# A recurrence's triangular inverse: levels one to four in 32x32 blocks, the last level as one corner block

## What is computed

```python
def wkv7_scan(r, decay, k, v, a_vec, b_vec):
    # S_t = S_{t-1} diag(w_t) + (S_{t-1} a_t) b_t^T + v_t k_t^T ;  y_t = S_t r_t
    def step(S, inp):
        r_t, w_t, k_t, v_t, a_t, b_t = inp
        sa = jnp.einsum('bhvk,bhk->bhv', S, a_t)
        S = S * w_t[:, :, None, :] + sa[..., :, None] * b_t[..., None, :] + v_t[..., :, None] * k_t[..., None, :]
        y = jnp.einsum('bhvk,bhk->bhv', S, r_t)
        return S, y
```

## Time and profile before

| | |
|---|---|
| median of 3 runs | 3347.98 us (3345.4 to 3358.46) |
| profiled execution, span from first to last instruction | 3342.9 us |
| the recurrence within it | 1762 to 2157 us |
| busy over the span: PE, DVE, ACT, POOL | 3046.9, 2026.2, 1103.6, 88.7 us |
| matmul records | 19562 |

### The profile page before, as it was taken

The page is one execution under the profiler, slowest core; times in us unless marked ns, Lnnn a source line. Parts: engine busy times, 40 slices in busy tenths (PEclk is TensorE's granted clock), DMA queues, the critical chain, the costliest instruction groups (busy, mean ns, idle before and its releaser), DMA issues.

```text
span 3342.9 us, 45792 instructions
## 1 busy us (share of the span) xinstructions
PE 3046.9 (91%) x19562; PEld 2487.4 (74%) x19565; DVE 2026.2 (61%) x3130; ACT 1103.6 (33%) x1684; POOL 88.7 (3%) x100
## 2 busy tenths in 40 slices
PE   6998899998998898995989888889999999889999
PEld 5876787786766787883767778768888777678887
DVE  5856795876577794876426777655353354554353
ACT  2334331223255431222324333342122444442121
POOL 0000000000000000000001121100000001000000
PEclk8998999998998999997999887889999999999999
DMA  8761453534621444541220000213332221023222
GB/s 238 170 182 35 166 195 133 189 129 148 204 75 45 170 158 143 178 153 51 84 46 10 12 7 12 70 62 101 101 95 94 77 88 51 7 76 101 95 94 88
DMA packets 236399, 345.55 MB, mean 103 GB/s; under 512 B 19604, under 2 KB 121948, under 8 KB 236196
## 3 DMA queue, kind: packets, MB, share of 16 engines
q1 hardware_dynamic: 217780, 327.27, 30.5%
q10 hardware_dynamic: 18416, 15.36, 1.7%
HBM read 340.45 MB, written 2.15 MB: 102 GB/s over the span
## 4 chain that ended last, share of the span: by engine, by line
PE 70%; DVE 18%; ACT 5%; DMA 5%; issue 1%; SPq 0%; DVEq 0%; ACTq 0%
PE bank L141 68%; DVE w_tiles L150 3%; DVE w_low L150 3%; DVE ada_acc L162 2%; PE bank L144 2%; ACT w_high L147 1%; DMA weight_ring<-in_f_w_down 1%; DMA first_ada<-in_w_ada 1%; ACT stage L147 1%; DVE x_natural L150 1%; DVE u_low L150 1%; DMA weight_ring<-in_d_w_in 1%; DMA weight_ring<-in_f_w_up 1%; DVE x_natural L162 1%; DVE stage L150 1%
## 5 line engine op out<-in xcount | busy, mean ns | idle before, releaser
L150 DVE TENSOR_TENSOR w_low<-weight_ring,w_high 128x2048 fp32r<-128x2048 f32 (+2 forms) x212 | 463.9, 2188 | 605.4 <-ACT w_high L147 605.4
L147 ACT ACTIVATE w_high<-weight_ring 128x2048 fp32r<-128x2048 f32 (+2 forms) x212 | 388.2, 1831 | 768.7 <-DMA weight_ring<-in_mlp_down 171.6
L141 PE MATMUL bank<-u_high,w_high 128*128 128x512 f32 x1472 | 582.9, 396 | 16.0 <-DVE u_low L150 5.9
L141 PE MATMUL bank<-u_high,w_low 128*128 128x512 f32 x1472 | 575.5, 391 | 0.0
L141 PE MATMUL bank<-u_low,w_high 128*128 128x512 f32 x1472 | 575.4, 391 | 0.0
L141 PE MATMUL bank<-w_high,u_high 128*128 128x512 f32 x896 | 354.0, 395 | 11.6 <-DVE u_low L150 6.7
L141 PE MATMUL bank<-w_low,u_high 128*128 128x512 f32 x896 | 350.4, 391 | 0.0
L141 PE MATMUL bank<-w_high,u_low 128*128 128x512 f32 x896 | 350.3, 391 | 0.0
L141 PEld LDWEIGHTS bank<-u_high,w_high 128*128 128x128 f32 x1472 | 278.0, 189 | 87.3 <-DVE u_low L150 19.1
L141 PEld LDWEIGHTS bank<-u_high,w_low 128*128 128x128 f32 x1472 | 277.7, 189 | 59.0
L141 PEld LDWEIGHTS bank<-u_low,w_high 128*128 128x128 f32 x1472 | 278.2, 189 | 55.8
(11 more groups left out here) (387 smaller groups left out, 4326.7 us busy)
## 6 DMA issues: line engine op xcount, KB each, us to landing
ada_ring<-in_mod_w SPq DMA_DIRECT2D x48, 1024.0 KB, 7.5
weight_ring<-in_f_w_up SPq DMA_DIRECT2D x44, 1024.0 KB, 5.1
ada_ring<-in_w_ada SPq DMA_DIRECT2D x40, 1024.0 KB, 7.3
weight_ring<-in_mlp_up SPq DMA_DIRECT2D x32, 1024.0 KB, 5.4
weight_ring<-in_mlp_down SPq DMA_DIRECT2D x32, 1024.0 KB, 5.0
weight_ring<-in_f_w_down SPq DMA_DIRECT2D x24, 768.0 KB, 4.7
weight_ring<-in_m_w_in SPq DMA_DIRECT2D x16, 1024.0 KB, 9.7
weight_ring<-in_d_w_in SPq DMA_DIRECT2D x12, 1024.0 KB, 5.3
```

The lines of the kernel that those rows point to most:

```text
L141: return self.e.matmul(out, l, r, start=start, stop=stop, skip_group_check=True)
L147: return self.e.activation(out, in_, f, **kw) if self.live else QUIET
L150: return self.e.tensor_tensor(out, a, b, op) if self.live else QUIET
```

## The change

Two facts of block matrices are used. The blocks of levels 0 to 4 never cross a border of 32 positions, so up to level 4 N, W and T hold nothing outside the diagonal 32x32 blocks. And level 5 joins two finished 32x32 blocks of a chunk by a single block, the upper right corner, which is all that is not zero in it.

After the change T, W, X, Bl and the masks are 32 columns wide instead of 64 (SB = 32), one 32x32 block in each strip of 32 partitions. A new tile `near` holds the diagonal blocks of N; DVE gathers it from G1 in two operations (the second half's columns times a column mask, then the first half's added). Levels 0 to 4 use `near`. A product of a level is sixteen matmuls of 32x32x32, `strips`, each on a diagonal strip of the array; the transposition t0 likewise. At level 5, PE multiplies the corner of G1 by T, from the lower strip of a chunk to the upper (`edges`, eight matmuls), and then X by W back. POOL places the 32x32 blocks of W into a tile `full` of 64 columns with zeros beside them, and DVE adds the corner to it. `w gh` reads `full`. POOL makes one mask fewer for each head and this placing instead. The number of steps in every generator, and so the order of the lists, stays as it was. `wkv_constants` has 708 columns instead of 834.

```diff
+SB = 32
+W_CONST = 3 * P + 8 * SB + HD + 4
...
+    strip = row // SB * SB + np.arange(SB)[None, :]
     up = []
-    for lv in range(6):
+    for lv in range(5):
         b = 1 << lv
         pair = (row // (2 * b) == col // (2 * b))
-        up.append(pair & (col % (2 * b) >= b) & (row % (2 * b) < b))
+        up.append(np.take_along_axis(pair & (col % (2 * b) >= b) & (row % (2 * b) < b), strip, axis=1))
     fold = lambda x: np.where(row[:, :] < CH, x[:, 0:CH], x[:, CH:P])
     stack = (row % HD == np.arange(HD)[None, :])
+    first, second = row % CH < SB, row % CH >= SB
+    halves = [np.repeat(first, SB, axis=1), np.repeat(second, SB, axis=1), first, second]
+    eye = (row % SB == np.arange(SB)[None, :])
     chunk = (row // CH == np.arange(2)[None, :])
-    wkv = [upto, same] + [fold(x) for x in [before, upto] + up] + [stack, chunk]
+    wkv = [upto, same] + [fold(x) for x in [before, upto]] + up + halves[0:2] + [eye, stack, chunk] + halves[2:4]
...
-        halves = lambda tile: (tile[:, 0:TT * CH], tile[:, TT * CH:])
+        parts = lambda tile: [chunks(tile[:, j * TT * SB:(j + 1) * TT * SB]) for j in range(4)]
         w.heads = []
         for h in range(2):
-            (T, W), Bl = halves(next(take)), halves(next(take))
-            w.heads.append(dict(G1=self.w_g[:, h, 0], G2=self.w_g[:, h, 1], T=chunks(T), W=chunks(W), Bl=[chunks(x) for x in Bl],
-                                X=next(take), R2=next(take)))
+            first, second = next(take), next(take)
+            T, W = parts(first)[0:2]
+            Bl, near = parts(second)[0:2], parts(second)[2]
+            w.heads.append(dict(G1=self.w_g[:, h, 0], G2=self.w_g[:, h, 1], T=T, W=W, Bl=Bl, near=near,
+                                full=chunks(first[:, TT * CH:]), X=next(take), R2=next(take)))
...
+        at = 3 * P
+        w.up = [cst[:, at + l * SB:at + (l + 1) * SB] for l in range(5)]
+        w.place, w.eye = cst[:, at + 5 * SB:at + 7 * SB], cst[:, at + 7 * SB:at + 8 * SB]
+        at += 8 * SB
+        w.stack, w.chunk = cst[:, at:at + HD], cst[:, at + HD:at + HD + 2]
+        w.first, w.second = cst[:, at + HD + 2:at + HD + 3], cst[:, at + HD + 3:at + HD + 4]
...
+        strips = [(t, slice(q, q + SB), slice(t * SB, t * SB + SB)) for t in range(TT) for q in range(0, P, SB)]
+        edges = [(t, slice(q, q + SB), slice(q + SB, q + 2 * SB), slice(t * SB, t * SB + SB)) for t in range(TT) for q in (0, CH)]
         for h, hd in enumerate(w.heads):
             pe.wait_ge(self.V, "w w", p, h, 0)
             if h in self.free:
                 pe.wait_ge(*self.free[h])
-            for t, c, at in blocks:
-                m = pe.matmul(self.bank[h][c, at], hd["W"][c, t, :], self.ident[c, c], True, True)
+            for t, r, at in strips:
+                m = pe.matmul(self.bank[h][r, at], hd["W"][r, t, :], self.ident[r, r], True, True)
             m.then_inc(*self.T.up("w t0", p, h))
             self.free[h] = (self.A, "w t0", p, h)
             yield
...
                     pe.wait_ge(self.V, "w t", p, h, l - 1)
-                pe.wait_ge(self.G, "w bl", p, h, l)
                 pe.wait_ge(*self.free[6 + h])
-                for t, c, at in blocks:
-                    m = pe.matmul(self.bank[6 + h][c, at], hd["Bl"][l % 2][c, t, :], hd["T"][c, t, :], True, True)
+                if l < 5:
+                    pe.wait_ge(self.G, "w bl", p, h, l)
+                    for t, r, at in strips:
+                        m = pe.matmul(self.bank[6 + h][r, at], hd["Bl"][l % 2][r, t, :], hd["T"][r, t, :], True, True)
+                else:
+                    pe.wait_ge(self.V, "w w", p, h, 4)
+                    for t, lo, hi, at in edges:
+                        m = pe.matmul(self.bank[6 + h][hi, at], hd["G1"][lo, t, 0, SB:CH], hd["T"][lo, t, :], True, True)
                 m.then_inc(*self.T.up("w x", p, h, l))
                 self.free[6 + h] = (self.A, "w x", p, h, l)
                 yield
             for h, hd in enumerate(w.heads):
-                X = chunks(hd["X"][:, 0:TT * CH])
+                X = chunks(hd["X"][:, 0:TT * SB])
                 pe.wait_ge(self.A, "w x", p, h, l)
                 pe.wait_ge(self.V, "w w", p, h, l - 1)
                 if l < 5:
                     pe.wait_ge(*self.free[h])
-                    for t, c, at in blocks:
-                        m = pe.matmul(self.bank[h][c, at], hd["W"][c, t, :], X[c, t, :], True, True)
+                    for t, r, at in strips:
+                        m = pe.matmul(self.bank[h][r, at], hd["W"][r, t, :], X[r, t, :], True, True)
                     m.then_inc(*self.T.up("w tx", p, h, l))
                     self.free[h] = (self.V, "w t", p, h, l)
-                for t, c, at in blocks:
-                    m = pe.matmul(self.bank[6 + h][c, at], X[c, t, :], hd["W"][c, t, :], True, True)
+                    for t, r, at in strips:
+                        m = pe.matmul(self.bank[6 + h][r, at], X[r, t, :], hd["W"][r, t, :], True, True)
+                else:
+                    for t, lo, hi, at in edges:
+                        m = pe.matmul(self.bank[6 + h][lo, at], X[hi, t, :], hd["W"][hi, t, :], True, True)
                 m.then_inc(*self.T.up("w wx", p, h, l))
                 self.free[6 + h] = (self.V, "w w", p, h, l)
...
-                m = pe.matmul(self.bank[h][c, ts(t)], hd["W"][c, t, :], hd["R2"][c, ts(t)], True, True)
+                m = pe.matmul(self.bank[h][c, ts(t)], hd["full"][c, t, :], hd["R2"][c, ts(t)], True, True)
...
-            a.activation(hd["T"], chunks(self.bank[h][:, 0:TT * CH]), ACT.Copy).then_inc(*self.A.up("w t0", p, h))
...
-                a.activation(hd["X"][:, 0:TT * CH], self.bank[6 + h][:, 0:TT * CH], ACT.Copy).then_inc(*self.A.up("w x", p, h, l))
...
-            v.tensor_tensor(hd["W"], hd["G1"][:, :, 0, :], spread(w.up[0]), ALU.mult).then_inc(*self.V.up())
+            v.tensor_scalar(hd["near"], hd["G1"][:, :, 0, SB:CH], w.second, None, ALU.mult).then_inc(*self.V.up())
             v.wait_ge(self.V)
-            v.tensor_tensor(hd["W"], hd["W"], spread(w.stack), ALU.add).then_inc(*self.V.up("w w", p, h, 0))
+            v.scalar_tensor_tensor(hd["near"], hd["G1"][:, :, 0, 0:SB], w.first, hd["near"], ALU.mult, ALU.add).then_inc(
+                *self.V.up("w near", p, h))
+            v.wait_ge(self.V)
+            if p:
+                v.wait_ge(self.G, "w full", p - 1, h)
+            v.tensor_tensor(hd["W"], hd["near"], spread(w.up[0]), ALU.mult).then_inc(*self.V.up())
+            v.wait_ge(self.V)
+            v.tensor_tensor(hd["W"], hd["W"], spread(w.eye), ALU.add).then_inc(*self.V.up("w w", p, h, 0))
             yield
...
-                    v.tensor_tensor(hd["T"], hd["T"], chunks(self.bank[h][:, 0:TT * CH]), ALU.add).then_inc(*self.V.up("w t", p, h, l))
+                    v.tensor_tensor(hd["T"], hd["T"], chunks(self.bank[h][:, 0:TT * SB]), ALU.add).then_inc(*self.V.up("w t", p, h, l))
                 v.wait_ge(self.T, "w wx", p, h, l)
                 v.wait_ge(self.V)
-                v.tensor_tensor(hd["W"], hd["W"], chunks(self.bank[6 + h][:, 0:TT * CH]), ALU.add).then_inc(*self.V.up("w w", p, h, l))
+                step = chunks(self.bank[6 + h][:, 0:TT * SB])
+                if l < 5:
+                    v.tensor_tensor(hd["W"], hd["W"], step, ALU.add).then_inc(*self.V.up("w w", p, h, l))
+                else:
+                    v.wait_ge(self.G, "w full", p, h)
+                    corner = hd["full"][:, :, SB:CH]
+                    v.scalar_tensor_tensor(corner, step, w.first, corner, ALU.mult, ALU.add).then_inc(*self.V.up("w w", p, h, l))
...
         for h, hd in enumerate(w.heads):
-            g.wait_ge(self.V, "w w", p, h, 0)
-            g.tensor_tensor(hd["Bl"][1], hd["G1"][:, :, 0, :], spread(w.up[1]), ALU.mult).then_inc(*self.G.up("w bl", p, h, 1))
+            g.wait_ge(self.V, "w near", p, h)
+            g.tensor_tensor(hd["Bl"][1], hd["near"], spread(w.up[1]), ALU.mult).then_inc(*self.G.up("w bl", p, h, 1))
             yield
         for l in range(1, 6):
             for h, hd in enumerate(w.heads):
-                if l < 5:
+                if l < 4:
                     if l > 1:
                         g.wait_ge(self.T, "w x", p, h, l - 1)
-                    elif p:
+                    g.tensor_tensor(hd["Bl"][(l + 1) % 2], hd["near"], spread(w.up[l + 1]), ALU.mult).then_inc(
+                        *self.G.up("w bl", p, h, l + 1))
+                elif l == 5:
+                    if p:
                         g.wait_ge(self.T, "w gh", p - 1, h)
-                    g.tensor_tensor(hd["Bl"][(l + 1) % 2], hd["G1"][:, :, 0, :], spread(w.up[l + 1]), ALU.mult).then_inc(
-                        *self.G.up("w bl", p, h, l + 1))
+                    g.wait_ge(self.V, "w w", p, h, 4)
+                    g.tensor_tensor(hd["full"].rearrange("p t (b s) -> p t b s", b=2),
+                                    hd["W"].unsqueeze(2).to_broadcast([P, TT, 2, SB]),
```

(14 more changed lines are left out.)

## The result

The changed kernel takes 3376.03 us (median of 4, 3374.53 to 3381.69) against 3346.69 for the kernel before (4 runs): ratio 1.0092, 95% interval 1.0075 to 1.0108. It is slower by 0.9%, where 0.9% faster was forecast, and lies above the forecast's range.

The account below looks back on a forecast made before the run. PE and DVE alternate: PE bounds levels 1 and 4 at 1.2 GHz, DVE most of the rest. Terms summed to 3.7 us a pair, 30 us for eight, giving 3318 us (chance 0.62); own range 3302 to 3337, overall 3302 to 3350.

Parts of the forecast that it names:

- Unit prices: PE in the recurrence: a burst of 32x32x32 products takes 0.27 us at 2.4 GHz, 0.45 at 1.2 GHz.
- rival (c): PE's bursts: matmuls start no faster than 29 ns apart, however small; a pair 3.8 us slower, 3378 us; chance 0.07.
- A change of shape: PE between state products and inverse: 0.1 us each, 14 added a pair, 5 on the path, 0.5 us.
- DVE's additions and its masking: DVE in a middle pair: 128x128 additions at 286 ns; masking, four operations of 128x128 for two of 128x256, loses 0.75 us.
- rival (d): DVE: 128x128 costs nearly what 128x256 does; 1.3 us gained a pair, 3338 us; chance 0.22 together with rival (a).
- columns halve: PE's bursts: halved columns, twice as many products side by side and doubled number give half the time if nothing else limits.
- Instructions: PE in the recurrence: 6656 more instructions; 7 us if issue waits grew with them, taken as 0, 7 kept for upper end.
- Rival (b): Score products and pair's end: clock stays low, 13 us more a pair, in half of the pairs; 3370 us; chance 0.09.
- Level 1: Level 1 of a middle pair, at 1.2 GHz: sums start 2.0 us earlier, 1.2 us of it kept as gain.
- rival (a): Each pair: one more 3.4 us stretch at 1.2 GHz; 1.5 us gain stays, 3336 us; chance 0.22 together with rival (d).
- The sum: Recurrence: terms of a middle pair add to 3.7 us gained, eight pairs 30 us, 3318 us of time.

Follow-up runs that it names:

- The split: Kernel before, each 64x64x64 product of t0 and levels 1 to 4 split into two of 64x32x64: 3369.36 us, 1.0065; with idle products, 3338.37 us, 0.9992.
- the fillers: Idle bf16 128x128x512 products where PE waits in the recurrence: added to the changed kernel 3373.45 us, 1.0085; to the kernel before 3311.19 us, 0.9903.
- its pair: Kernel before, inverse products in one pass of upper halves, with idle products: 3321.33 us, with more 3307.26 us; changed kernel done likewise: 3329.0 and 3324.21 us.

## Why the prediction was wrong

**Unit prices: right in the main.** PE ran four bursts (x128) in 1.93 us at 1.2 GHz and two (x64) in 0.75 us at 2.4 (above): less the last matmul's 0.22 that is 0.43 and 0.27 a burst, where 0.45 and 0.27 were taken. So rival (c), a floor of 29 ns from start to start, is out: 32 matmuls in 0.27 us are 8 ns each. With it goes the floor of about 25 ns in the Trainium skill, TensorE: Matmul & The Clock Gate, section "Wait — 56ns, not 53.3ns?", for matmuls that run on different tiles. A change of shape cost about the 0.1 us taken for it at 2.4 GHz, and up to 0.15 at 1.2. DVE's additions and its masking, after:

```profile
L156 DVE TENSOR_TENSOR w_tiles<-w_tiles,bank 128x128 f32<-128x128 f32 x128 | 36.8, 287 | 66.1 <-PE bank L147 54.8 <-DVE w_tiles L156 0.5
...
L156 DVE TENSOR_TENSOR w_tiles<-w_tiles,w_const 128x128 f32<-128x128 f32 x32 | 11.5, 358 | 1.1
```

287 ns against 286 for the additions, so rival (d) is out as well. The masking is somewhat dearer: 358 ns for two of its four operations, where 0.32 was taken with the gap. But the right column of the first row is the case: these additions save 0.13 us each and stand 54.8 us for PE, where 172 additions of double width stood 25.7.

**The columns: right number, half the reason.** The burst was halved because "columns halve". Half the columns on the same 64x64 tiles gave nothing (2.00 us for four bursts against 2.06). Halving the output rows instead, with all 64 columns kept, took a matmul from 29 to 14 ns, and 32x32 tiles took it to 8. A smaller tile has less to load for each product and lets more products run side by side; which of the two counts, and how much fewer columns add in the last step, 14 to 8, is not shown. The Trainium skill, TensorEngine Tiling (Array Packing), section Instruction Overhead, says that a matmul with one column takes as long as one with 60, and the prediction had concluded from it that a burst would stay near 0.46 us. The run with half the columns agrees with the page; the conclusion drawn for the burst does not hold, since it took 0.27 us.

**The failed step: "Instructions".** "If these waits grew with the instructions, 46% more would bring 7 us; I take 0". Both the value and the law were wrong. The waits are not a share of the instructions but what is missing to some 3.5 us when 256 instructions are used up sooner. Before, a level's bursts took 2 to 3.6 us for 64 matmuls and 64 loads, so blocks came at 7 us on the mean (57 in 395 us), never closer than 3.92, and only 2.1 us of gaps showed; after, 256 instructions are four bursts, 1.1 to 1.7 us. The demand could have been worked out from the forecast's own burst, 0.27 us for 64 instructions: a block each 1.1 us, where the trace had none under 3.92. The limit itself, 3.3 us, is in no row of the kernel before. Gaps of 45.6 us came. The split cost 22 to 30 us, changes of shape included, and the changed kernel got 44 us back when its gaps went: the size of the whole forecast gain or more.

**The second failed step: the clock.** Rival (b), 3370 with a chance of 0.09, is the mechanism that came, beside supply, and more broadly than it was drawn. That its time lies so near the measured 3376 is luck: it had nothing for supply in it. The score products, 3.09 us at 2.4 GHz before, after (the first row; the second is the window from them to the transpositions):

```profile
1926.57 5.33 PE L147 MATMUL bank<-w_art,w_tiles 64*64 64x128 f32 x58 [1.74 <-DVE w_tiles L171]
```
```profile
1926.50:1933.40 6.90, 6.81 (x100) 6.54 (x100) 4.29 (x11) 0.00 (x0) 0.56 (x1) 0.54 0.09 20
```

The first masking therefore waits 2.47 us for them instead of 1.19. Level 1, where 1.2 us a pair were to be gained, stood at 1.2 GHz from the transpositions to its end, in a stretch that is 17.06 us long where it was 10.24:

```profile
1927.05:1944.11 17.06, 14.67 (x348) 13.64 (x344) 10.07 (x25) 4.75 (x9) 3.32 (x6) 0.50 0.03 8
```

The prediction had the right evidence, that PE is dense over level 1 and still needed 10.24 us to leave 0.50, but used it for rival (a) alone, with one more stretch of 3.4 us a pair; here the stretch grew by 6.8, and in the whole window the time at 1.2 GHz went from 123 to 280 us. The size of such a loss is shown by the run with half the columns, 50 us at nearly the same mean clock, 0.69.

**The sum.** Forecast -30; the split +22 to +30; measured +31 (0.92% of 3346). If the forecast gain were there in full and the costs simply added, the clock would have cost 31 to 39 us, which the half-columns run allows. Neither is shown. The costs don't simply add: in the changed kernel the fillers took 136 us off the time at 1.2 GHz and only 3 us off the whole, where in the kernel before 91 us less brought 33. And with supply nearly out of the way the changed layout stayed 8 and 17 us behind its pair at slightly lower clocks. How much of this is clock, and how much the longer masking and the waits between engines in the levels, stays open. So two causes are shown, each by a run of its own, and their shares are not.

**The range.** It was also narrower than its own terms. With every term at its good end a pair gains 7.0 us, not the 5.8 behind the 3302; with every term at its bad end it loses 0.7, which is 3354, or 3361 with the 7 us kept for instructions, and the forecast's own range stopped at 3337. The measured time is outside even that.

## What to carry to other kernels

Count PE's instructions against time as well as its columns: where 256 matmuls and loads were used up in under 3.5 us, cutting products smaller bought nothing here, and "issue" waits of over 1 us in the midst of a burst, at one position of each 256, are the sign. Where PE and another engine alternate, less work on PE can lower its clock for what follows, as it did here; idle products in its waits brought 1% here, which no smaller block did. Try the split alone and the fillers alone before a layout is rewritten, and count the changes of tile shape that each adds.

## What the hardware showed that was not expected

- One 16 KB packet of instructions for each 256 of PE's, never closer than 3.3 us (3.34, 3.32, 3.30 in three kernels), though each packet took only 0.9 to 1.4 us in the changed kernel; in a series 3.68 us on the mean from block to block. Why they come no closer is not shown.
- In a series of 32x32 products, of which gaps for instructions took half the time, the clock went from 1.00 to 0.51. In the split kernel, with 29.5 us of such gaps, it stayed at 0.86.
- Half the columns on 64x64 tiles left a burst as long as it was (2.00 us for four against 2.06 at 2.4 GHz) and the clock of the window at 0.69 instead of 0.86.
- At 2.4 GHz a matmul started every 8 ns on four 32x32 tiles side by side, every 14 ns on 64x32 and every 29 ns on 64x64; halved columns on 64x64 tiles saved nothing.
- A change of tile shape cost about 0.1 us at 2.4 GHz and up to 0.15 us at 1.2 GHz, from start to start.
